# VectorE's convolution taps accumulate in two PSUM banks instead of two SBUF rows

## The chip, the cores and the metric

The kernel runs on one core of a Trainium2 chip. The metric is the device time of one execution in microseconds (us), the median of three runs. Engines are called by the names of the profile: PE is TensorE's matmul, PEld its weight load, DVE is VectorE, ACT is ScalarE, POOL is GpSimd, SP issues most DMAs.

## The reference

One decoder layer over 512 prompt tokens and 8 x 4 sampled tokens, 544 columns in all, model width 2048. An RMSNorm and one input projection give two groups. Group A is attention over keys that an indexer picks. Group B is a Conformer convolution module over 1024 channels; then an output projection, a SwiGLU FFN and a final norm. What the change touches is group B:

```python
def conformer_conv(u, conv_prev, conv_dw, conv_dw_bias, conv_ln_g, conv_ln_b):
    a, gate = jnp.split(u, 2, axis=-1)
    g = a * jax.nn.sigmoid(gate)
    buf = jnp.concatenate([conv_prev.astype(g.dtype), g], axis=1)
    y = lax.conv_general_dilated(buf, conv_dw[:, None, :].astype(buf.dtype), window_strides=(1,),
                                 padding='VALID', dimension_numbers=('NWC', 'WIO', 'NWC'),
                                 feature_group_count=CONV_WIDTH)
    y = jax.nn.silu(layer_norm(y + conv_dw_bias, conv_ln_g, conv_ln_b))
    return y, buf[:, -(CONV_KERNEL - 1):]
```

The convolution is depthwise and causal, 31 taps wide: each output column is the sum of 31 shifted columns of `g`, each times a weight of its channel. All data is fp32.

## The kernel before

Activations lie transposed, channels on partitions and tokens in the free dimension. Every weight tile (1024 rows by 128 columns, a "unit") is loaded by SP into one of four slots of `raw`, split by ScalarE into a high part (`whi`, L587) and by VectorE or GpSimd into the remainder (`wlo`, L848 and L516), and multiplied by TensorE in three products per half, 48 matmuls of 272 columns a unit (`unit`, L1346). A tile of 128 output channels is two units, and a pair is two tiles. Slot 0 of the accumulators is PSUM banks 0 and 1, slot 1 banks 2 and 3. ScalarE and the remainder work one pair ahead of TensorE.

The stage around the change runs over the eight blocks of 128 convolution channels (c = 0 to 7). Every engine has its own program, and semaphores join them.

- TensorE: for block i the first tile of the pair P_U + i (the values), then `new_state(i - 1)`, a transpose of the tile `tg` (L1477), then the second tile (the gates). It waits for `s_tg` before the transpose. After block 7 come the pairs P_Q (with the last transpose between its tiles), P_Q + 1, and then the column sums for the LayerNorm (L1494), which wait for all taps (`s_conv`).
- VectorE, `u_step(c)`: scale the values out of PSUM into `ga` (L1057); taps 0 to 9 of block c - 1 (`taps`, L1017 to L1024); scale the gates into `sg` (L1057), after a wait for TensorE's second tile; `convolved(c - 1)`, that is taps 10 to 20, the row sums of GpSimd's products for the sampled tokens (L1032, L1034), and two adds that join the partial sums (L1037, L1040); `gated(c)`, which writes the new `gbuf` and ends with `tg` (L1046 to L1054); one round of the sampled tokens' top-k (L1066 to L1069). The loop runs c = 1 to 7. The taps of block 7 lie in `rope_pair(P_Q)`, between and behind the two ropes. Before the loop there are seven top-k rounds.
- The 31 taps of a block are divided: VectorE has ND = 21 and ScalarE and GpSimd have NA = 10. ScalarE makes the product of one tap (L683, into `y2` or `tap`), GpSimd adds it to `y2` (L526, nine adds). GpSimd also makes the products of the sampled tokens (L534) and four remainders per block (L516), in between the adds, in the order of `conv_step`.
- VectorE's taps alternate between two accumulators, even taps in the row of `y` and odd ones in `y3`, both in SBUF. Tap k waits until tap k - 2 is complete (`s_conv`). Taps 0 and 1 are a multiply of `gbuf` with the weight, tap 0 with the bias added; the others are one instruction each, accumulator = `gbuf` shifted by k, times weight, plus accumulator (L1024).
- PSUM in this stage: banks 0 to 3 accumulate, bank 6 takes the transposes of `tg`. Banks 4 and 5 are used before it (the transposed old state, copied out by ScalarE, `s_stc`) and after it (the LayerNorm's squares, L1501).

Of the kernel before, what the change touches and what calls it, by code (L numbers as in the profile page):

```python
# [14 lines left out]
F32 = mybir.dt.float32  # L15
# [3 lines left out]
ALU = mybir.AluOpType  # L19
# [3 lines left out]
P = 128  # L23
D = 2048
SEQ = 512
# [24 lines left out]
NA = 10  # L50
# [66 lines left out]
def build(nc, a, o):  # L117
    with ExitStack() as ctx:
# [7 lines left out]
        def at(name, shape, dt, offset):  # L126
            return nc.alloc_sbuf_tensor_at(name, shape, dt, offset=base + offset)
# [10 lines left out]
        vec = at("vec", [P, 56], F32, C0 + 1280)  # L138
        cw = at("cw", [P, CT, CK], F32, C0 + 1504)
        stat = at("stat", [P, 64], F32, C0 + 2496)  # L140
        S0 = C0 + 2816
# [48 lines left out]
        gbuf = at("gbuf", [P, SEQ + CK - 1 + B * (CK - 1 + T)], F32, R0)  # L190
        y = at("y", [P, CT, NT], F32, R0 + 3264)
# [5 lines left out]
        cout = at("cout", [CK - 1 + NS, CW_], F32, S0 + 26880)  # L197
        tapS = at("tapS", [P, B, T, CK], F32, S0 + 17408)
        y2 = at("y2", [P, SEQ], F32, S0 + 21760)
        y3 = at("y3", [P, SEQ], F32, S0 + 23936)  # L200
        tap = at("tap", [P, 2, SEQ], F32, S0 + 49728)
        vT = at("vT", [P, NKV, NT], F32, S0 + 49728)
        kN = at("kN", [P, 5, 256], F32, S0 + 38848)
# [637 lines left out]
        def _(dve):  # L841
# [166 lines left out]
            ch.link(ve.tensor_copy(scK[:, :], scS[:, :]))  # L1008
            ve.memset(gbuf[:, 0:CK - 1], 0.0).then_inc(s_xs, 1)

            def taps(c, k0, k1):

                yp = y[:, bass.ds(c, 1), 0:SEQ].rearrange("p a n -> p (a n)")
                for k in range(k0, k1):
                    wk = cw[:, bass.ds(c, 1), k]
                    if k == 0:
                        ve.tensor_scalar(yp, gbuf[:, 0:SEQ], wk, vec[:, bass.ds(32 + c, 1)], ALU.mult, ALU.add  # L1017
                                         ).then_inc(s_conv, 1)
                    elif k == 1:
                        ve.tensor_scalar(y3[:, :], gbuf[:, 1:1 + SEQ], wk, None, ALU.mult).then_inc(s_conv, 1)  # L1020
                    else:
                        dst = y3[:, :] if k % 2 else yp
                        dve.wait_ge(s_conv, CN * c + k - 1)
                        ve.scalar_tensor_tensor(dst, gbuf[:, k:k + SEQ], wk, dst, ALU.mult, ALU.add  # L1024
                                                ).then_inc(s_conv, 1)

            def convolved(c):
# [6 lines left out]
                ve.tensor_scalar(ys, ys, vec[:, bass.ds(32 + c, 1)], None, ALU.add).then_inc(s_ssum, 1)  # L1034
                yp = y[:, bass.ds(c, 1), 0:SEQ].rearrange("p a n -> p (a n)")
                dve.wait_ge(s_conv, CN * c + ND)
                ve.tensor_tensor(yp, yp, y3[:, :], ALU.add).then_inc(s_conv, 1)  # L1037
                dve.wait_ge(s_conv, CN * c + ND + 1)
                dve.wait_ge(s_add, (NA - 1) * c + NA - 1)
                ve.tensor_tensor(yp, yp, y2[:, :], ALU.add).then_inc(s_conv, 1)  # L1040

            def gated(c):

# [687 lines left out]
```

## Time and profile before

| | |
|---|---|
| median of 3 runs | 2850.33 us (2847.47 to 2851.39) |
| profiled execution | 2844.5 us |
| its span | 2842.8 us |
| busy in the span: PE, PEld | 2613.4 us (92%), 2447.4 us (86%) |
| DVE, ACT, POOL | 1289.6 us (45%), 828.6 us (29%), 433.0 us (15%) |
| mean granted TensorE clock | 0.962 of full speed |
| chain that ended last, by engine | PE 79%, DVE 9%, issue 7% |

The span is the profiled execution without what lies around its first and last instruction, 1.7 us here. The convolution stage is from about 310 to 636 us of it and the FFN from about 1100 us to the end. A row of a timeline may stand for several equal instructions, with their count at its end; its second number then is from the start of the first to the end of the last. In brackets stands the idle time of the engine before it and who ended that.

### The profile page before, as it was taken

How to read it: one execution, taken by the hardware profiler on the slowest of the kernel's cores; microseconds unless marked ns; L12 is line 12 of the kernel's file. 1: busy time of each engine (PE TensorE's matmuls, PEld its weight loads, DVE VectorE, ACT ScalarE, POOL GpSimd, SP SyncE). 2: the span in 40 equal slices, each digit the busy share in tenths (PEclk: the TensorE clock that was granted, in tenths of full speed). 3: DMA queues.
4: the chain of work that ended last, by engine and by line, in shares of the span. 5: the costliest groups of instructions: out<-in, count | busy, mean ns of one | idle time of the engine just before them, and what ended most of it. 6: DMA issues, size and time to landing. Idle time of an engine off the chain costs nothing.

```text
span 2842.8 us, 50617 instructions
## 1 busy us (share of the span) xinstructions
PE 2613.4 (92%) x19388; PEld 2447.4 (86%) x19390; DVE 1289.6 (45%) x1750; ACT 828.6 (29%) x1052; POOL 433.0 (15%) x439
## 2 busy tenths in 40 slices
PE   5977877669889899999999999999999999999997
PEld 5952877669754479999999999999999999999997
DVE  5577599996561223343333333333333333333333
ACT  5143233222341212243332233322333322222222
POOL 3302477665323300000000000000000000000000
PEclk8988988889999999999999999999999999999999
DMA  7403222122325533423322333223322223333232
GB/s 223 110 3 87 60 56 55 52 78 56 91 86 162 158 101 108 132 77 89 89 70 84 104 89 89 85 67 89 105 88 83 76 81 100 90 88 89 68 89 98
DMA packets 424178, 256.01 MB, mean 90 GB/s; under 512 B 19915, under 2 KB 413235, under 8 KB 422752
## 3 DMA queue, kind: packets, MB, share of 16 engines
q1 hardware_dynamic: 412176, 225.88, 27.4%
q0 software_dynamic: 11936, 29.30, 3.5%
q8 instruction: 36, 0.59, 0.1%
q14 instruction: 30, 0.25, 0.0%
HBM read 244.70 MB, written 11.27 MB: 90 GB/s over the span
## 4 chain that ended last, share of the span: by engine, by line
PE 79%; DVE 9%; issue 7%; ACT 2%; DMA 1%; DVEq 1%; POOLq 0%; POOL 0%; SPq 0%; ACTq 0%
PE ps L1346 70%; DVE y L1024 2%; PE ps L1597 2%; PE ps L1626 2%; PE ps L1574 1%; DVE scP L957 1%; PE ps L1452 1%; DVE scS L1069 1%; PE ps L1428 0%; DVE m L1066 0%; DVE y L1017 0%; PE ps L1554 0%; ACT whi L587 0%; DVE stat L1207 0%; PE ps L1443 0%
## 5 line engine op out<-in xcount | busy, mean ns | idle before, releaser
L848 DVE TENSOR_TENSOR wlo<-raw,whi 128x1024 fp32r<-128x1024 f32 (+1 forms) x358 | 437.6, 1223 | 1192.5 <-ACT whi L587 1191.9
L1346 PE MATMUL ps<-xhi,whi 128*128 128x272 f32 (+1 forms) x4512 | 944.6, 291 | 15.0 <-DVE wlo L848 7.5
L1346 PE MATMUL ps<-xhi,wlo 128*128 128x272 f32 (+1 forms) x4512 | 939.0, 290 | 0.0
L1346 PE MATMUL ps<-xlo,whi 128*128 128x272 f32 (+1 forms) x4512 | 938.7, 290 | 0.0
L587 ACT CAST whi<-raw 128x1024 fp32r<-128x1024 f32 (+1 forms) x410 | 429.2, 1047 | 1286.0 <-PE ps L1346 1199.0
L1346 PEld LDWEIGHTS ps<-xhi,whi 128*128 128x128 f32 (+1 forms) x4512 | 715.9, 190 | 17.2 <-issue 10.8
L1346 PEld LDWEIGHTS ps<-xlo,whi 128*128 128x128 f32 (+1 forms) x4512 | 716.6, 190 | 0.0
L1346 PEld LDWEIGHTS ps<-xhi,wlo 128*128 128x128 f32 (+1 forms) x4512 | 711.6, 190 | 0.0
L1346 PE MATMUL ps<-hidh,whi 128*128 128x272 f32 x1408 | 291.4, 288 | 4.6 <-DVE hidl L1300 4.6
L1346 PE MATMUL ps<-hidl,whi 128*128 128x272 f32 x1408 | 290.9, 288 | 0.0
L1346 PE MATMUL ps<-hidh,wlo 128*128 128x272 f32 x1408 | 290.8, 288 | 0.0
L1346 PEld LDWEIGHTS ps<-hidh,whi 128*128 128x128 f32 x1408 | 219.5, 188 | 5.5 <-issue 5.5
L1346 PEld LDWEIGHTS ps<-hidl,whi 128*128 128x128 f32 x1408 | 219.7, 188 | 0.0
L1346 PEld LDWEIGHTS ps<-hidh,wlo 128*128 128x128 f32 x1408 | 219.6, 188 | 0.0
L1024 DVE SCALAR_TENSOR_TENSOR y<-gbuf,cw,y 128x512 f32<-128x512 f32 (+1 forms) x152 | 206.5, 1426 | 0.0
L516 POOL TENSOR_TENSOR wlo<-raw,whi 128x1024 fp32r<-128x1024 f32 x52 | 135.9, 2618 | 52.2 <-ACT whi L587 52.2
L526 POOL TENSOR_TENSOR y<-y,tap 128x512 f32<-128x512 f32 x72 | 112.3, 1559 | 3.5
L683 ACT ACTIVATE tap<-gbuf,cw 128x512 f32<-128x512 f32 x72 | 52.0, 722 | 98.3 <-POOL y L526 98.0
L1477 PE MATMUL ps<-ident,tg 128*128 128x128 f32 x8 | 3.6, 447 | 79.6 <-DVE tg L1054 79.6
L1477 PEld LDWEIGHTS ps<-ident,tg 128*128 128x128 f32 x8 | 1.4, 178 | 81.1 <-issue 68.9
L350 POOL DMA_DIRECT2D idxN<-in_cache_idx_k x96 | 51.7, 539 | 102.4 <-issue 101.5
L820 ACT CAST hidh<-ut 128x544 f32 x44 | 28.5, 647 | 128.5 <-DVE ut L1298 128.5
(278 smaller groups left out, 1752.3 us busy)
## 6 DMA issues: line engine op xcount, KB each, us to landing
raw<-in_w_gate SPq DMA_DIRECT2D x88, 512.0 KB, 3.8
raw<-in_w_up SPq DMA_DIRECT2D x88, 512.0 KB, 3.8
raw<-in_w_in SPq DMA_DIRECT2D x72, 512.0 KB, 3.8
raw<-in_w_down SPq DMA_DIRECT2D x64, 384.0 KB, 3.3
raw<-in_w_down SPq DMA_DIRECT2D x64, 320.0 KB, 3.1
raw<-in_w_out SPq DMA_DIRECT2D x32, 512.0 KB, 5.3
ring_pages<-in_cache_k SPq DMA_DIRECT2D x48, 128.0 KB, 2.7
ring_pages<-in_cache_k POOLq DMA_DIRECT2D x48, 128.0 KB, 3.1
```

Source lines behind the costliest of these rows:

```text
L350: eng.dma_start(idxN[:, b % IB, bass.ds(g, 1), :].rearrange("p a d -> p (a d)"), ic[bass.ds(pg, 1), :, :].rearrange("a s d -> (a s) d")).t ...
L516: nc.gpsimd.tensor_tensor(wlo[:, u.slot, :, :], raw[:, u.slot, :, :], whi[:, u.slot, :, :].bitcast(F32), ALU.subtract).then_inc(s_lo, 1)
L526: nc.gpsimd.tensor_tensor(y2[:, :], y2[:, :], tap[:, (k - 1) % 2, :], ALU.add).then_inc(s_add, 1)
L587: nc.scalar.copy(whi[:, u.slot, :, 0:cols], raw[:, u.slot, :, 0:cols]).then_inc(s_hi, 1)
L683: nc.scalar.activation(dst, gbuf[:, ND + k:ND + k + SEQ], ACT.Copy, scale=cw[:, bass.ds(c, 1), ND + k]).then_inc(s_tap, 1)
L820: nc.scalar.copy(tile_of(hidh, j), halves(ut[:, :])).then_inc(s_hh, 1)
L848: ve.tensor_tensor(wlo[:, u.slot, :, 0:cols], raw[:, u.slot, :, 0:cols], whi[:, u.slot, :, 0:cols].bitcast(F32), ALU.subtract).then_inc(s_ ...
L957: ve.scalar_tensor_tensor(dst, rel[:, n % 2, 0:SW[i]], wiP[:, i, hh:hh + 1], dst, ALU.mult, ALU.add).then_inc(s_ia, 1)
L1024: ve.scalar_tensor_tensor(dst, gbuf[:, k:k + SEQ], wk, dst, ALU.mult, ALU.add).then_inc(s_conv, 1)
L1346: ins = te.matmul(ps[0:cols, 2 * slot + half, 0:HALF], w[:, u.slot, t, 0:cols], x[:, k0 + t, HALF * half:HALF * half + HALF], start=(hf == ...
L1597: ins = te.matmul(ps[r0:r0 + 32, c, :], qpad[:, b, kv, :], kpT[:, q % 2, kv, :], start=False, stop=True, skip_group_check=True)
L1626: ins = te.matmul(ps[r0:r0 + 32, 7, 0:256], pST[:, 4 * (j % 4) + k, r0:r0 + 32], page_slot(n)[:, k, :], start=(j % 4 == 0 and k == 0), sto ...
```

## The change

The row `y3` goes. The even taps accumulate in PSUM bank 4 and the odd taps in bank 5. The two adds at the end change places: first odd taps plus `y2` into the row of `y`, after a wait for GpSimd's adds, and then even taps plus that row.

```diff
-        y3 = at("y3", [P, SEQ], F32, S0 + 23936)
...
+            even_taps, odd_taps = ps[:, 4, 0:SEQ], ps[:, 5, 0:SEQ]
+
             def taps(c, k0, k1):
 
-                yp = y[:, bass.ds(c, 1), 0:SEQ].rearrange("p a n -> p (a n)")
                 for k in range(k0, k1):
                     wk = cw[:, bass.ds(c, 1), k]
                     if k == 0:
-                        ve.tensor_scalar(yp, gbuf[:, 0:SEQ], wk, vec[:, bass.ds(32 + c, 1)], ALU.mult, ALU.add
+                        ve.tensor_scalar(even_taps, gbuf[:, 0:SEQ], wk, vec[:, bass.ds(32 + c, 1)], ALU.mult, ALU.add
                                          ).then_inc(s_conv, 1)
                     elif k == 1:
-                        ve.tensor_scalar(y3[:, :], gbuf[:, 1:1 + SEQ], wk, None, ALU.mult).then_inc(s_conv, 1)
+                        ve.tensor_scalar(odd_taps, gbuf[:, 1:1 + SEQ], wk, None, ALU.mult).then_inc(s_conv, 1)
                     else:
-                        dst = y3[:, :] if k % 2 else yp
+                        dst = odd_taps if k % 2 else even_taps
                         dve.wait_ge(s_conv, CN * c + k - 1)
                         ve.scalar_tensor_tensor(dst, gbuf[:, k:k + SEQ], wk, dst, ALU.mult, ALU.add
                                                 ).then_inc(s_conv, 1)
...
                 dve.wait_ge(s_conv, CN * c + ND)
-                ve.tensor_tensor(yp, yp, y3[:, :], ALU.add).then_inc(s_conv, 1)
+                dve.wait_ge(s_add, (NA - 1) * c + NA - 1)
+                ve.tensor_tensor(yp, odd_taps, y2[:, :], ALU.add).then_inc(s_conv, 1)
                 dve.wait_ge(s_conv, CN * c + ND + 1)
-                dve.wait_ge(s_add, (NA - 1) * c + NA - 1)
-                ve.tensor_tensor(yp, yp, y2[:, :], ALU.add).then_inc(s_conv, 1)
+                ve.tensor_tensor(yp, even_taps, yp, ALU.add).then_inc(s_conv, 1)
```

The order of VectorE's program at the end of a block, in `convolved` and the start of `gated`, before the change (`y_113` is `y3`, `y_112` is `y2`, a wait stands in brackets):

```order
L1034 TENSOR_SCALAR y<-y,vec 128x32 [waits s_ssum]
L1036 REGISTER_ALU
L1037 TENSOR_TENSOR y<-y,y_113 128x512 [waits s_conv]
L1038 REGISTER_ALU
L1039 ISA [waits s_conv]
L1040 TENSOR_TENSOR y<-y,y_112 128x512 [waits s_add]
L1045 REGISTER_ALU
L1046 ISA [waits s_conv]
L1046 COPY gbuf<-stT 128x8x30
```

The same place in the changed kernel (`ps` is PSUM):

```order
L1034 TENSOR_SCALAR y<-y,vec 128x32 [waits s_ssum]
L1036 REGISTER_ALU
L1037 ISA [waits s_conv]
L1038 ISA [waits s_add]
L1038 TENSOR_TENSOR y<-ps,y_112 128x512
L1039 REGISTER_ALU
L1040 TENSOR_TENSOR y<-ps,y 128x512 [waits s_conv]
L1045 REGISTER_ALU
L1046 ISA [waits s_conv]
L1046 COPY gbuf<-stT 128x8x30
```

The wait for GpSimd's adds stands ahead of the first of the two adds instead of the second. Nothing else changes its place on any engine; the taps keep their order and change only their operands.

## Rows read from the trace of the kernel before

**Rows 1.** Waits of TensorE, 357 to 588 us: who waited for whom, total, times, longest

```profile
PE ps L1477 <- DVE tg L1054: 67.6, 6, 12.7
```

**Rows 2.** Stretches: length; busy PE, PEld, DVE, ACT, POOL (instructions); clock; DMA share; GB/s

```profile
357.00:395.50 38.50, 27.11 (x193) 26.87 (x193) 37.55 (x38) 11.50 (x16) 27.79 (x17) 0.81 0.21 55
...
1100.00:2800.00 1700.00, 1690.18 (x13474) 1688.64 (x13473) 581.51 (x604) 495.26 (x502) 0.00 (x0) 1.00 0.30 88
```

**Rows 3.** Timeline of VectorE, one step: start, length, line, instruction

```profile
395.27 0.17 DVE L1054 COPY tg<-gbuf 128x32 f32<-128x32 f32 x1
...
398.34 1.53 DVE L1017 TENSOR_SCALAR y<-gbuf,cw,vec 128x512 f32 x1
399.79 2.62 DVE L1020 TENSOR_SCALAR y<-gbuf,cw 128x512 f32<-128x512 f32 x1
402.33 15.91 DVE L1024 SCALAR_TENSOR_TENSOR y<-gbuf,cw,y 128x512 f32 x8
418.17 0.71 DVE L1057 TENSOR_TENSOR sg<-ps,rstd 128x544 f32<-128x544 f32 x1
418.80 10.93 DVE L1024 SCALAR_TENSOR_TENSOR y<-gbuf,cw,y 128x512 f32 x11
429.66 1.17 DVE L1032 TENSOR_REDUCE y<-tapS 128x992 f32 x1
...
431.02 0.68 DVE L1037 TENSOR_TENSOR y<-y,y 128x512 f32 x1
...
433.79 0.17 DVE L1054 COPY tg<-gbuf 128x32 f32<-128x32 f32 x1
```

**Rows 4.** Timeline of VectorE, first step of the loop (taps 0, 1, 2 to 9)

```profile
336.80 2.25 DVE L1017 TENSOR_SCALAR y<-gbuf,cw,vec 128x512 f32 x1
338.96 0.47 DVE L1020 TENSOR_SCALAR y<-gbuf,cw 128x512 f32<-128x512 f32 x1
339.36 5.38 DVE L1024 SCALAR_TENSOR_TENSOR y<-gbuf,cw,y 128x512 f32 x8
```

**Rows 5.** Timeline of GpSimd, same two steps

```profile
336.39 2.36 POOL L516 TENSOR_TENSOR wlo<-raw,whi 128x1024 fp32r<-128x1024 f32 x1
...
395.72 2.62 POOL L534 TENSOR_TENSOR tapS<-gbuf,cw 128x248 f32<-128x248 f32 x4 [10.36 <-DVE tg L1054]
...
415.95 5.17 POOL L526 TENSOR_TENSOR y<-y,tap 128x512 f32<-128x512 f32 x3
421.09 2.80 POOL L516 TENSOR_TENSOR wlo<-raw,whi 128x1024 fp32r<-128x1024 f32 x1
```

**Rows 6.** Timeline of VectorE, first rope add of P_Q

```profile
592.23 2.83 DVE L916 TENSOR_TENSOR qT<-qT,rt 128x544 f32<-128x544 f32 x1
```

**Rows 7.** Groups of VectorE by line and shape: count, busy us, mean ns

```profile
L1310 DVE TENSOR_TENSOR h<-ps,h 128x544 f32 x62 | 44.4, 716 | 0.0
...
L1298 DVE TENSOR_TENSOR ut<-ut,gt 128x544 f32<-128x544 f32 x44 | 31.9, 726 | 7.9 <-DVE ut L1295 6.6
...
L1207 DVE TENSOR_REDUCE stat<-ps 128x1 f32<-128x512 f32 x8 | 5.5, 689 | 5.2 <-PE ps L1536 5.2
...
L1207 DVE TENSOR_REDUCE stat<-ps 128x1 f32<-128x128 f32 x8 | 2.3, 287 | 0.1
```

**Rows 8.** Single lines: shortest, median and longest duration in ns

```profile
L1024 DVE SCALAR_TENSOR_TENSOR y<-gbuf,cw,y x152: 729/1156/5904, 339.4 to 632.6; 128x512 f32<-128x512 f32 x82, 128x512 f32 x70
...
L526 POOL TENSOR_TENSOR y<-y,tap x72: 1263/1628/1768, 317.1 to 611.6; 128x512 f32<-128x512 f32 x72
...
L516 POOL TENSOR_TENSOR wlo<-raw,whi x52: 2357/2578/2872, 293.2 to 730.1; 128x1024 fp32r<-128x1024 f32 x52
```

**Rows 9.** Timeline of TensorE after the transpose of `tg`

```profile
395.79 0.82 PE L1346 MATMUL ps<-xhi,whi 128*128 128x272 f32 x2
```

**Rows 10.** Timeline of TensorE after the convolution: column sums, next pair

```profile
636.06 9.27 PE L1494 MATMUL ps<-y,ones 128*128 128x272 f32 x32 [7.81 <-DVE y L1040]
646.57 0.52 PE L1346 MATMUL ps<-xhi,whi 128*128 128x272 f32 x2 [1.24 <-DVE rt L913]
```

## The prediction

> **What bounds the kernel now.** I began with the waits of TensorE in the stretch of the convolution. Between 357 and 588 us it waits for one thing, the tile `tg` that VectorE's gated() writes: six times, 67.6 us in all [rows 1]. The table of stretches then shows the two sides of one step (one channel block, about 38.5 us): VectorE is busy 37.55 us of it, TensorE 27.11 us, and TensorE's granted clock is 0.81 there, against 1.00 in the FFN [rows 2]. So VectorE sets the length of a step and TensorE waits. The step is read from VectorE's timeline: from `tg` to the next `tg` is 433.79 - 395.27 = 38.52 us, of which the first ten taps take 398.34 to 418.17 and the other eleven 418.80 to 429.66 [rows 3].
>
> The taps are what is slow. In the first step of the loop GpSimd's last instruction ends at 338.75, and taps 2 to 9, from 339.36 on, take 5.38 us, 0.67 us each [rows 4, 5]. In a steady step GpSimd works (2.62 us of products at 395.72, then adds and weight remainders until 423.9) and the same eight taps take 15.91 us, 2.0 us each [rows 3, 5]. A tap reads `gbuf` and its accumulator, both in SBUF. At 418.17 VectorE runs `sg<-ps,rstd`, one operand of which is in PSUM, in the middle of three GpSimd adds (415.95 to 421.12), and it takes 0.71 us, as ever [rows 3, 5]. At 592.23 a rope add with both operands in SBUF takes 2.83 us [rows 6]; alone such an instruction takes 0.73 [rows 7]. So an instruction with two SBUF tensors waits for GpSimd's, and one with a single SBUF tensor does not. The Trainium skill (SBUF — State Buffer, "Who interferes with whom") says that VectorE's second SBUF input comes through a port shared with GpSimd, held for a whole instruction, the loser blocked; by that rule the trace agrees, 2.0 us against 0.67.
>
> **The change, part by part.** Taps 2 to 20 keep one operand in SBUF (`gbuf`) and move the other, with the result, to PSUM banks 4 and 5. No instruction is added or removed. No other engine touches those banks between the last state copy and the squares of the LayerNorm.
>
> *Price of a tap, p.* No row shows VectorE writing PSUM. The nearest, an add that reads PSUM and SBUF, takes 0.716 us for 544 columns, the same with both in SBUF 0.726 [rows 7]: reading PSUM is free. The low end is 0.67 us, the tap without GpSimd [rows 4]; a gain on that is excluded, since its 512 columns take the time that they take in any row, PSUM or SBUF. In the middle lies 0.73, the shortest duration recorded of one tap [rows 8]: now a tap starts 0.06 us before the one ahead of it has ended, and in PSUM it might not. The high end is 1.2 us, if reading and writing one bank take turns: from 128 to 512 columns a reduction out of PSUM goes from 0.287 to 0.689 us [rows 7], so 512 columns are worth 0.53 us, which would come twice. I take p = 0.70, between the two that it resembles most, since reading PSUM shows no price; 1.2 stays as a rival. The Trainium skill (VectorE: DVE Perf Modes, "The TRN2 errata") gives a VectorE instruction from PSUM 62 cycles more than one from SBUF, an estimate of 0.065 us a tap. By it p would be 0.735 and the kernel some 3 us slower than my sum; the two adds of [rows 7] show nothing of it, and no row here has a write to PSUM. Taps 0 and 1 read only `gbuf` plus scalars; they took 1.5 and 2.6 us beside GpSimd [rows 3]. I price them at p too.
>
> *The new steady step*, counted from the end of `tg` (395.44 in rows 3):
> - TensorE's second tile starts 0.35 us after it (395.79) [rows 9] and has 96 matmuls. At full clock one takes 1690.18 / 13474 = 0.1254 us [rows 2], so 12.0 us; with 0.2 us until VectorE sees it, `sg` can be read at 12.6.
> - VectorE reaches its first tap at 2.9 (398.34) and ends ten at 2.9 + 10p = 9.9. It now waits 2.7 us for TensorE, a wait that the old trace does not have.
> - `sg` 0.63, eleven taps 11p = 7.7: at 20.9. The sum of the sampled products and its bias take 431.02 - 429.66 = 1.36: at 22.3 the two adds begin. From there to the end of `tg` takes 433.96 - 431.02 = 2.94.
> - Together 17.5 + 11p = 25.2 us.
>
> *What is late next.* GpSimd must have made its nine adds by 22.3: it starts at 0.3, then 2.6 for the products, 9 x 1.26, and three remainders of 2.36 by their shortest durations [rows 5, 8]: 21.3. The add wait is moved ahead of both sums instead of one, but it has 1.0 us to spare. The last remainder ends at 23.7, before the copies into `gbuf` at 24.0, so these don't collide. TensorE needs 0.35 + 192 x 0.1254 = 24.4: it waits 0.8 us a step. ScalarE has 11.50 us of work a step [rows 2] and its products only follow GpSimd's adds. The weight loads, a DMA share of 0.21 over 38.5 us, become 0.32 over 25.2, what the FFN holds without a wait (0.30) [rows 2]. Three engines within a microsecond: below 24.4 the step cannot go.
>
> *Sum.* Steps 2 to 7: 6 x (38.52 - 25.2) = 79.9 us. TensorE enters the first of them from the idle time before tg(1) at the lower clock: after a wait of 11 us (67.6 / 6) [rows 1] its first pair of matmuls takes 0.82 us [rows 9], against 0.52 after a short wait [rows 10], which makes 27.11 us out of 24.4 with the transpose [rows 2]; that costs 2.7 once. The first step gains 1.6 on tap 0 (2.25 now) and loses 0.2 on tap 1 (0.47 now) and 19 x 0.03 on the rest: 0.8 [rows 4]. After tg(7) at 588.0 the last block lies between the two ropes of P_Q. TensorE runs P_Q's second tile to 600.5, P_Q+1 to 624.6 at full clock, no longer held by the second rope; VectorE begins the taps 7 us after tg(7), as now: the first rope's add keeps its two SBUF operands and its wait [rows 6]. Ten taps bring it to 602, the second rope with such an add (some 4.7) to 606.7, eleven taps to 614.4, product sums and adds (1.4 + 1.4) to 617. So the 7.81 us wait at 636.06 goes [rows 10], the column sums start at 624.6, take 9.3 and end at 633.9. VectorE needs 646.57 - 636.06 = 10.5 us from the end of its sums until its top-k rounds and the rope have freed bank 0 [rows 10], so that is at 628 and in time. P_Q+2 starts at 633.9 where it started at 646.57: 12.7 us. Behind it the same engines wait for each other in the same order, up to an FFN bound by TensorE, so nothing gives this back.
>
> 0.8 + 79.9 - 2.7 + 12.7 = 90.7 us. The profiled execution took 2844.5 us, so 2753.8; the median of the three runs is 5.8 above it, so 2759.6, say **2759 us**.
>
> **The rivals.**
> 1. *TensorE's clock does not recover* (or GpSimd turns out 2 us late). For it: it was 0.81 in the step of [rows 2]. Against: the falls follow waits of 11 us, and a wait of 1.24 us at 646.57 is followed by a pair of matmuls in 0.52 us where after the long wait it took 0.82 [rows 9, 10]. If each short wait cost the 2.7 us, the step is 28 us and the kernel 6 x 2.7 = 16 slower: 2775.
> 2. *PSUM in place is slow,* p = 1.2. Then VectorE is the chain throughout: 7.8 + 21p = 33.0 a step, 33 us gained there, about 9 behind tg(7), 9.6 lost in the first step, which has no GpSimd to hide from: 2850 - 32 = 2818. For it: no row has such a write. Against: reading PSUM costs nothing.
> 3. *Slower: the taps stay blocked.* Every tap also reads a per-partition scalar of `cw` from SBUF. If that read, and not the second tensor, is what waits for GpSimd, taps take as long as now, (418.17 - 398.34 + 429.66 - 418.80) / 21 = 1.46 us on average [rows 3], and each is longer by what PSUM adds to it, 0.06 us at p = 0.73: 21 x 8 blocks x 0.06 = 10 us, so 2860. It decides from p = 1.46, where 7.8 + 21p reaches 38.5. Against: ropes and `sg` do not show it, but they have no such scalar.
> 4. *The change does nothing*, the taps not being on the path: 2850. Rows 1 and 2 speak plainly against it.
>
> **How the numbers follow.** The forecast has 0.80, rival 1 has 0.08, rival 2 0.06, rival 3 0.05, rival 4 0.01. The forecast's own range: p from 0.67 to 0.73 gives steps of 24.9 to 25.5 and TensorE's floor 24.4, so 2754 to 2761, and with 4 us for the tail and the spread of runs 2749 to 2768. To hold rival 1 the range goes up to 2780 and leaves out rivals 2 to 4, 0.12. Measured differences under 0.2% (5.7 us) are no change: same is 0.01, slower 0.05 by rival 3, faster 0.94.
>
> **What would show it.** In the new profile taps of 0.67 to 0.75 us in every step; VectorE waiting about 2.7 us for TensorE before `sg`; GpSimd's adds at 1.27 us instead of 1.6, since nothing makes them wait either; `tg` every 25 us; TensorE's granted clock near 1 from 395 us on; no wait before the column sums; and the end moved by what the stretch up to 650 us gained. Taps over 1 us would prove rival 2 (the same length in the first step) or 3 (short in the first step, long later). A step of 28 us with TensorE's clock at 0.8 is rival 1. I am wrong if the step shortens and the end does not follow.

## The result and the profile after

| | before | after |
|---|---|---|
| median | 2848.9 us (2847.05 to 2851.39, 4 runs) | 2758.12 us (2757.81 to 2762.01, 4 runs) |
| profiled execution, its span | 2844.5, 2842.8 us | 2758.33, 2756.6 us |
| busy PE | 2613.4 us (92%) | 2605.8 us (95%) |
| busy DVE, POOL | 1289.6, 433.0 us | 1177.1, 404.3 us |
| mean granted TensorE clock | 0.962 | 0.975 |
| `tg(1)` to `tg(7)` | 231.1 us | 154.1 us |

The ratio is 0.9684 (0.9667 to 0.9701): 90.8 us less by the medians, where 90.7 were forecast, and 0.9 us from the forecast time. As a difference of the two profiled executions it is 86.2 us. That these are two numbers is part of the explanation below. The kernel before stands at 2850.33 us in the table of its own profile, by three runs; a fourth, of 2847.05 us, brings its median to 2848.9.

The costliest groups of the changed kernel's page, those of the taps and of GpSimd's adds (busy us, mean ns of one, idle time before):

```profile
L1024 DVE SCALAR_TENSOR_TENSOR ps<-gbuf,cw,ps 128x512 f32<-128x512 f32 x152 | 101.5, 748 | 0.0
L525 POOL TENSOR_TENSOR y<-y,tap 128x512 f32<-128x512 f32 x72 | 94.2, 1308 | 3.5
```

All 152 taps now last between 741 and 755 ns, where the old ones went from 729 to 5904 [rows 8]. GpSimd's adds got shorter as well, 1308 ns on average (median 1304) after a median of 1628: the two engines had been holding each other up.

One step of VectorE in the changed kernel, `tg` to `tg`, which answers to [rows 3]. It is 405.85 - 380.43 = 25.42 us long:

```profile
380.43 0.17 DVE L1054 COPY tg<-gbuf 128x32 f32<-128x32 f32 x1
...
383.50 0.81 DVE L1017 TENSOR_SCALAR ps<-gbuf,cw,vec 128x512 f32<-128x512 f32 x1
384.22 0.75 DVE L1020 TENSOR_SCALAR ps<-gbuf,cw 128x512 f32<-128x512 f32 x1
384.87 5.36 DVE L1024 SCALAR_TENSOR_TENSOR ps<-gbuf,cw,ps 128x512 f32<-128x512 f32 x8
393.28 0.72 DVE L1057 TENSOR_TENSOR sg<-ps,rstd 128x544 f32<-128x544 f32 x1 [3.05 <-PE ps L1346]
393.92 7.33 DVE L1024 SCALAR_TENSOR_TENSOR ps<-gbuf,cw,ps 128x512 f32<-128x512 f32 x11
...
402.37 0.24 DVE L1034 TENSOR_SCALAR y<-y,vec  x1
402.67 0.69 DVE L1038 TENSOR_TENSOR y<-ps,y 128x512 f32 x1
403.39 0.69 DVE L1040 TENSOR_TENSOR y<-ps,y 128x512 f32 x1
404.23 0.78 DVE L1046 COPY gbuf<-stT 128x240 f32 x1
...
405.85 0.17 DVE L1054 COPY tg<-gbuf 128x32 f32<-128x32 f32 x1
```

The eight taps that took 15.91 us take 5.36. Taps 0 and 1 are short too, although they read one SBUF tensor as before and only their result has moved. Tap 1 in all eight blocks, before and after (shortest, median, longest in ns):

```profile
L1020 DVE TENSOR_SCALAR y<-gbuf,cw x8: 475/2610/2617, 339.0 to 596.4; 128x512 f32<-128x512 f32 x8
```

```profile
L1020 DVE TENSOR_SCALAR ps<-gbuf,cw x8: 737/744/747, 335.4 to 515.4; 128x512 f32<-128x512 f32 x8
```

Before `sg` VectorE waits 3.05 us for TensorE. GpSimd in the same step, for [rows 5]:

```profile
380.88 2.64 POOL L533 TENSOR_TENSOR tapS<-gbuf,cw 128x248 f32<-128x248 f32 x4 [3.07 <-DVE tg L1054]
...
387.08 4.06 POOL L525 TENSOR_TENSOR y<-y,tap 128x512 f32<-128x512 f32 x3
...
398.46 4.06 POOL L525 TENSOR_TENSOR y<-y,tap 128x512 f32<-128x512 f32 x3
402.48 2.39 POOL L515 TENSOR_TENSOR wlo<-raw,whi 128x1024 fp32r<-128x1024 f32 x1
```

Its ninth add is through at 402.5 and VectorE's first sum starts at 402.67: these two are as good as level. And the last remainder, 402.48 to 404.87, lies over the copy at 404.23, which takes 0.78 us instead of 0.28.

Waits of TensorE from 357 to 510 us, where 67.6 us stood before [rows 1], and the stretch of one step for [rows 2]:

```profile
PE ps L1477 <- DVE tg L1054: 5.0, 6, 0.9
```

```profile
381.50:406.90 25.40, 24.51 (x195) 24.23 (x194) 21.48 (x38) 11.38 (x18) 23.59 (x18) 1.00 0.26 66
```

TensorE is busy 24.51 of 25.40 us at full clock. VectorE is no longer the fullest engine (21.48); GpSimd (23.59) is fuller than it.

### The profile page after: what moved, and what is told of

It is laid out like the page before. It is cut to its first block, busy times and chain, and to the rows that moved or that the text cites. A ratio compares the mean times of both kernels' runs of the same rounds, so it can differ in the third digit from the quotient of the medians.

```text
span 2756.6 us, 50626 instructions
## 1 busy us (share of the span) xinstructions
PE 2605.8 (95%) x19390; PEld 2438.2 (88%) x19390; DVE 1177.1 (43%) x1750; ACT 827.7 (30%) x1052; POOL 404.3 (15%) x439
## 4 chain that ended last, share of the span: by engine, by line
PE 86%; DVE 6%; issue 3%; ACT 2%; DMA 1%; POOL 1%; DVEq 0%; SPq 0%; POOLq 0%; ACTq 0%
PE ps L1346 76%; PE ps L1597 2%; PE ps L1626 2%; PE ps L1574 1%; DVE scP L956 1%; POOL y L525 1%; PE ps L1452 1%; PE ps L1428 1%; DVE ps L1024 1%; PE ps L1554 0%; PE ps L1443 0%; ACT whi L586 0%; ACT idxT L651 0%; PE ps L1536 0%; DVE stat L1207 0%
## 5 line engine op out<-in xcount | busy, mean ns | idle before, releaser
L515 POOL TENSOR_TENSOR wlo<-raw,whi 128x1024 fp32r<-128x1024 f32 x52 | 125.4, 2416 | 49.2 <-ACT whi L586 49.2
L1024 DVE SCALAR_TENSOR_TENSOR ps<-gbuf,cw,ps 128x512 f32<-128x512 f32 x152 | 101.5, 748 | 0.0
L525 POOL TENSOR_TENSOR y<-y,tap 128x512 f32<-128x512 f32 x72 | 94.2, 1308 | 3.5
L1597 PE MATMUL ps<-kpT,qpad 128*32 128x512 f32 x128 | 62.6, 615 | 0.0
L1250 DVE COPY kpT<-ps 128x512 f32<-128x512 f32 x32 | 22.1, 691 | 71.4 <-PE ps L1574 71.4
```

The costliest lines, as they stand in the source:

```text
L515: nc.gpsimd.tensor_tensor(wlo[:, u.slot, :, :], raw[:, u.slot, :, :], whi[:, u.slot, :, :].bitcast(F32), ALU.subtract).then_inc(s_lo, 1)
L525: nc.gpsimd.tensor_tensor(y2[:, :], y2[:, :], tap[:, (k - 1) % 2, :], ALU.add).then_inc(s_add, 1)
L1597: ins = te.matmul(ps[r0:r0 + 32, c, :], qpad[:, b, kv, :], kpT[:, q % 2, kv, :], start=False, stop=True, skip_group_check=True)
```

## The experiments

**One operand at a time.** The prediction rested on one statement: what makes a tap slow is the second *read* from SBUF, and not the write to SBUF. The change moves both. The first two runs move one each.

`e1_read_psum`, made from the changed kernel: the taps read their accumulator in PSUM and write to the rows in SBUF. They no longer accumulate; the sum over the taps is left out.

```diff
+        y3 = at("y3", [P, SEQ], F32, S0 + 23936)
...
+                yp = y[:, bass.ds(c, 1), 0:SEQ].rearrange("p a n -> p (a n)")
...
-                        ve.scalar_tensor_tensor(dst, gbuf[:, k:k + SEQ], wk, dst, ALU.mult, ALU.add
+                        row = y3[:, :] if k % 2 else yp
+                        ve.scalar_tensor_tensor(row, gbuf[:, k:k + SEQ], wk, dst, ALU.mult, ALU.add
...
-                ve.tensor_tensor(yp, odd_taps, y2[:, :], ALU.add).then_inc(s_conv, 1)
+                ve.tensor_tensor(yp, yp, y3[:, :], ALU.add).then_inc(s_conv, 1)
...
-                ve.tensor_tensor(yp, even_taps, yp, ALU.add).then_inc(s_conv, 1)
+                ve.tensor_tensor(yp, yp, y2[:, :], ALU.add).then_inc(s_conv, 1)
```

> Made from the changed kernel. Taps 2 to 20 read their second operand from PSUM but write their result to the SBUF rows of before, so they do not accumulate: the sum over the taps is left out, the number and size of the instructions is not. Theory A (what waits for GpSimd is the second SBUF tensor that is read): taps of 0.67 to 0.75 us beside GpSimd, a step of 25 to 26 us, 2756 to 2762 us. Rival theory B (what waits is the write of the result to SBUF, or a write to SBUF and a read from it together): taps of 1.4 to 2.0 us on average, a step of 38 us, about 2850 us.

2764.36 us, ratio 0.9713 (0.9685 to 0.9741). VectorE in a step:

```profile
396.41 7.32 DVE L1027 SCALAR_TENSOR_TENSOR y<-gbuf,cw,ps 128x512 f32 x11
...
405.12 2.85 DVE L1041 TENSOR_TENSOR y<-y,y 128x512 f32 x1
```

Taps that write SBUF are as short as those of the change: all 152 last between 731 and 747 ns. The step is 27.05 us, above the 25 to 26 expected and the change's 25.4, because this kernel's sum of the two rows reads two SBUF tensors again: it starts beside GpSimd's last remainder and takes 2.85 us.

`e2_write_psum`, the reverse, made from the kernel before: taps 2 to 20 read the rows in SBUF and write PSUM. The sum over the taps is left out here too, and the two adds stand as in the changed kernel.

```diff
+            even_taps, odd_taps = ps[:, 4, 0:SEQ], ps[:, 5, 0:SEQ]
...
-                        dst = y3[:, :] if k % 2 else yp
+                        dst = odd_taps if k % 2 else even_taps
                         dve.wait_ge(s_conv, CN * c + k - 1)
-                        ve.scalar_tensor_tensor(dst, gbuf[:, k:k + SEQ], wk, dst, ALU.mult, ALU.add
+                        row = y3[:, :] if k % 2 else yp
+                        ve.scalar_tensor_tensor(dst, gbuf[:, k:k + SEQ], wk, row, ALU.mult, ALU.add
...
-                ve.tensor_tensor(yp, yp, y3[:, :], ALU.add).then_inc(s_conv, 1)
+                dve.wait_ge(s_add, (NA - 1) * c + NA - 1)
+                ve.tensor_tensor(yp, odd_taps, y2[:, :], ALU.add).then_inc(s_conv, 1)
                 dve.wait_ge(s_conv, CN * c + ND + 1)
-                dve.wait_ge(s_add, (NA - 1) * c + NA - 1)
-                ve.tensor_tensor(yp, yp, y2[:, :], ALU.add).then_inc(s_conv, 1)
+                ve.tensor_tensor(yp, even_taps, yp, ALU.add).then_inc(s_conv, 1)
```

> The mirror image: taps 2 to 20 read their second operand from the SBUF rows and write to the PSUM banks; the sum over the taps is left out here too. Theory A: the taps wait for GpSimd as before, 2.0 us each while it runs, a step of 38 to 39 us, about 2850 us. Theory B: taps of 0.67 to 0.75 us and 2756 to 2762 us. If a write to PSUM costs something of its own, it shows in the first step, where GpSimd is idle: over 0.67 us a tap there.

2847.99 us, ratio 0.9995 (0.9984 to 1.0006): nothing is left of the gain. Its first step, which has no GpSimd beside it, and a later one:

```profile
339.14 5.39 DVE L1027 SCALAR_TENSOR_TENSOR ps<-gbuf,cw,y 128x512 f32<-128x512 f32 x8
...
401.98 15.94 DVE L1027 SCALAR_TENSOR_TENSOR ps<-gbuf,cw,y 128x512 f32<-128x512 f32 x8
```

15.94 us, as before the change [rows 3], with the result in PSUM. The first step has them in 5.39 us, so the write to PSUM costs nothing by itself. Both runs together: for an instruction with two tensor inputs, the gain is in the read.

**Half of the taps.** `e3_odd_only`: only the odd taps have PSUM, the even ones stay in `y`.

```diff
-                        ve.tensor_scalar(even_taps, gbuf[:, 0:SEQ], wk, vec[:, bass.ds(32 + c, 1)], ALU.mult, ALU.add
+                        ve.tensor_scalar(yp, gbuf[:, 0:SEQ], wk, vec[:, bass.ds(32 + c, 1)], ALU.mult, ALU.add
...
-                        dst = odd_taps if k % 2 else even_taps
+                        dst = odd_taps if k % 2 else yp
...
-                ve.tensor_tensor(yp, odd_taps, y2[:, :], ALU.add).then_inc(s_conv, 1)
+                ve.tensor_tensor(yp, odd_taps, yp, ALU.add).then_inc(s_conv, 1)
...
-                ve.tensor_tensor(yp, even_taps, yp, ALU.add).then_inc(s_conv, 1)
+                ve.tensor_tensor(yp, yp, y2[:, :], ALU.add).then_inc(s_conv, 1)
```

> Half of the change: the odd taps accumulate in PSUM bank 5, the even ones in the row of y as before. Theory A: every second tap still waits for GpSimd and delays one of its instructions in turn; the other runs in its shadow. Even taps of 1.2 to 2 us, odd ones of 0.75 us, the first ten taps in about 10 to 13 us instead of 20; a step of 28 to 32 us, 2775 to 2805 us. Rival (no lock, but the two accumulators in neighbouring SBUF rows disturb each other, so that one in PSUM is enough): all taps short and 2758 us.

2803.24 us, ratio 0.985 (0.9821 to 0.9878), a step of 31.1 us. Even and odd taps in one step, and the bias of the sampled row:

```profile
391.20 2.22 DVE L1025 SCALAR_TENSOR_TENSOR y<-gbuf,cw,y 128x512 f32 x1
393.35 0.74 DVE L1025 SCALAR_TENSOR_TENSOR ps<-gbuf,cw,ps 128x512 f32<-128x512 f32 x1
394.01 1.12 DVE L1025 SCALAR_TENSOR_TENSOR y<-gbuf,cw,y 128x512 f32 x1
...
412.17 2.36 DVE L1035 TENSOR_SCALAR y<-y,vec  x1
```

All even and all odd taps of the run:

```profile
L1025 DVE SCALAR_TENSOR_TENSOR y<-gbuf,cw,y x80: 736/1124/7690, 337.7 to 579.0; 128x512 f32 x70, 128x512 f32<-128x512 f32 x10
L1025 DVE SCALAR_TENSOR_TENSOR ps<-gbuf,cw,ps x72: 741/743/751, 338.3 to 578.3; 128x512 f32<-128x512 f32 x72
```

Side by side in one step, the odd taps take 0.74 us and the even ones 1.12 or more, but for one of 0.74 that began 0.11 us ahead of a GpSimd add. A per-partition scalar from `cw` stands in both, so it is not what waits. The bias L1035 is a surprise that returns below: this instruction has a single SBUF tensor as its input, and it waited too.

**The other side of the contention.** `e4_short_adds`: the kernel before, with GpSimd's adds cut to one of 512 columns (their sum is left out).

```diff
-                    nc.gpsimd.tensor_tensor(y2[:, :], y2[:, :], tap[:, (k - 1) % 2, :], ALU.add)
+                    nc.gpsimd.tensor_tensor(y2[:, 0:1], y2[:, 0:1], tap[:, (k - 1) % 2, 0:1], ALU.add)
```

> Made from the kernel before, with VectorE's taps in SBUF. GpSimd's nine adds per block are cut to one column each, with all their waits and signals; their sum is left out for the other 511 columns. The remainders and the sampled products stay. Theory A: only the taps that meet a remainder (four of 2.4 us per block) wait; a step of 25 to 29 us, 2765 to 2790 us. Rival (the taps are slow in SBUF for a reason other than GpSimd): a step of 36 us or more and over 2830 us.

2789.96 us, ratio 0.9803 (0.9773 to 0.9833). The old taps (shortest, median, longest in ns):

```profile
L1024 DVE SCALAR_TENSOR_TENSOR y<-gbuf,cw,y x152: 733/741/2897, 336.4 to 562.2; 128x512 f32<-128x512 f32 x82, 128x512 f32 x70
```

Without touching VectorE's program the median tap falls from 1156 to 741 ns and the step to 29.9 us, where 25 to 29 were expected. What is left to the changed kernel's step, 4.5 us, goes with taps beside the remainders: eight taps take 9.68 us at 389.92, with two remainders among them, against 5.36. So it is GpSimd's instructions that made the taps slow.

**The add order.** `e5_early_wait`: the kernel before, with the changed order of the two adds and its earlier wait alone.

```diff
-                ve.tensor_tensor(yp, yp, y3[:, :], ALU.add).then_inc(s_conv, 1)
-                dve.wait_ge(s_conv, CN * c + ND + 1)
                 dve.wait_ge(s_add, (NA - 1) * c + NA - 1)
-                ve.tensor_tensor(yp, yp, y2[:, :], ALU.add).then_inc(s_conv, 1)
+                ve.tensor_tensor(y3[:, :], y3[:, :], y2[:, :], ALU.add).then_inc(s_conv, 1)
+                dve.wait_ge(s_conv, CN * c + ND + 1)
+                ve.tensor_tensor(yp, yp, y3[:, :], ALU.add).then_inc(s_conv, 1)
```

> The other part of the change alone, in the kernel before: accumulators stay in SBUF, but the wait for GpSimd's adds stands ahead of the first of the two sums, which now adds y2 to the odd row. Theory: GpSimd is done some 8 us before VectorE comes to the sums, so the earlier wait costs nothing: 2849 us, within 3 us of the kernel before. Rival: the earlier wait or the other order of the sums is worth something by itself: 2840 us or less, or 2855 us or more.

2849.42 us, ratio 1.0006 (0.9996 to 1.0015): in the kernel before, the order and the earlier wait are worth nothing. What the earlier wait costs in the changed kernel, where GpSimd's ninth add ends just ahead of the first sum, this run can't show.

**Who sets the new step?** `e6_split14`: the changed kernel with 14 instead of 10 taps ahead of `sg`, so that VectorE works in the 3 us in which it waits.

```diff
-                taps(c, ND // 2, ND)
+                taps(c, 14, ND)
...
-                     mid=(lambda: taps(c - 1, 0, ND // 2)) if conv else None, lows=False)
+                     mid=(lambda: taps(c - 1, 0, 14)) if conv else None, lows=False)
...
-            rope_pair(P_Q, qT, 0, 9, c1, s1, HD, mid=lambda: taps(CT - 1, 0, ND // 2), lows=False)
+            rope_pair(P_Q, qT, 0, 9, c1, s1, HD, mid=lambda: taps(CT - 1, 0, 14), lows=False)
```

> The changed kernel, with 14 instead of 10 taps ahead of the wait for TensorE's second tile, and 7 behind it. They fit into the 3.05 us that VectorE waits there. Theory (GpSimd's adds end with VectorE's last tap, both chains decide): VectorE is ready 2.6 us earlier and waits for GpSimd instead; a step still of 25.2 to 25.4 us, 2757 to 2759 us. Rival (VectorE's taps behind TensorE's tile are the only chain): a step down to TensorE's 24.4 us, 6 us less: 2752 us.

2758.14 us, ratio 0.9691 (0.9678 to 0.9704), a step of 25.37 us: no gain. VectorE comes to the bias L1034 2.6 us earlier, is held there for up to 1.36 us (three of the six steps have the usual 0.24), and then waits for GpSimd at its first sum (waits from 357 to 510 us):

```profile
DVE y L1038 <- POOL y L525: 10.9, 5, 2.7
```

GpSimd sets the end of the step as much as VectorE does.

`e7_na9` takes a tap from ScalarE and GpSimd instead and gives it to VectorE.

```diff
-NA = 10
+NA = 9
```

> The changed kernel with one tap moved from ScalarE and GpSimd (NA 9 for 10) to VectorE (22 for 21), 11 ahead of TensorE's tile, 11 behind it as now. Theory: GpSimd ends 1.37 us earlier, its last remainder no longer stands in the way of the copy into gbuf (0.5 us), VectorE's chain stays: a step of 24.8 us, 3 to 4 us less, 2754 to 2755 us. Rival (only VectorE's chain): no change, 2758 us; if the tap more costs VectorE its 0.66 us on the path, 2762 us.

2760.09 us, ratio 0.9697 (0.9684 to 0.9711), a step of 25.65 us, where 24.8 and 2754 to 2755 us were expected. This was a miss. GpSimd is 1.4 us sooner at its last remainder, 402.69 for a `tg` at 382.06, and VectorE runs into that:

```profile
404.00 1.11 DVE L1034 TENSOR_SCALAR y<-y,vec  x1
```

0.24 us in the changed kernel's steady steps, 1.10 to 1.16 here in five steps. The bias of 32 columns has one tensor input, in SBUF, and its result in SBUF, and it waits for GpSimd to end.

`e8_na9_split14` is both edits together.

> Both edits together: 22 taps on VectorE, 14 ahead of TensorE's tile and 8 behind, GpSimd with eight adds. Theory: both chains end before TensorE is ready, TensorE waits for tg no longer, a step of 24.4 us from the third on: 6 us less than the changed kernel, 2752 us. If a third chain holds the step (ScalarE, the weight loads), it stays above 24.8 us and the time at 2754 us or more.

2749.76 us, ratio 0.9654 (0.9641 to 0.9668): 8.4 us faster than the change. Its short steps are 24.0 us (402.96 to 426.95 to 450.98), in which TensorE never waits: that is 192 matmuls at 0.125 us, and less than the 24.4 that the prediction and this run's theory took for the floor. Two of the six steps are longer. The first is 25.67 us: TensorE enters it after a wait of 5.74 us, and its granted clock over it is 0.92. The fifth is 25.71 us at full clock: in it the bias L1034 takes 2.44 us beside a remainder. The next experiment is about the first of these causes, the last three about the second.

**The start of the stage.** What still held TensorE was VectorE's late arrival at the first `ga` and `tg(1)` (waits of 3.0 and 5.2 us in the changed kernel). `e9_early3`, made from `e8_na9_split14`, starts 3 rounds of the sampled top-k before the loop instead of 7 and does the other four later.

```diff
-EARLY = 7
+EARLY = 3
...
-            topk_sample(R1, 3)
-            R1 += 3
+            topk_sample(R1, 5)
+            R1 += 5
             rope_pair(P_K, kT, 0, 17, c1, s1, HD, lows=False)
-            topk_sample(R1, 3)
-            R1 += 3
+            topk_sample(R1, 5)
+            R1 += 5
```

> The run before it (nine taps on GpSimd, fourteen of VectorE's taps ahead of sg, steps of 24.0 us), and in addition only 3 steps of the later side work are begun ahead of the convolution instead of 7, and two samples behind it take 5 steps each instead of 3. Theory (what still holds TensorE at the start of the first stage is VectorE coming late to ga(1) and tg(1)): VectorE comes to ga(1) some 10 us sooner, TensorE no longer waits 3.0 us for ga and 5.2 us for tg(1), and does not fall to the low clock there; 10 to 12 us less than the run before, so 2738 to 2742. Rival (the work that was begun early is wanted later, and its delay holds up the rotary embedding and attention): what the first stage gains is given back there, 2748 or more. Second rival: the moved work stands inside the steps on VectorE, each step longer than 24.0 us; then tg(1) to tg(7) is over 146 us and the time about 2745 to 2750.

2740.29 us, ratio 0.9618 (0.9604 to 0.9631), 9.5 us less than the run before it and inside the first theory's 2738 to 2742. `tg(0)` to `tg(1)` fell from 41.2 to 30.3 us, and 1.6 us of it is given back between `tg(7)` and the sampled attention. The first step, 345.44 to 371.16, is still 25.72 us long: in it the bias L1034 takes 2.36 us. All waits of TensorE for `tg` from 300 to 620 us:

```profile
PE ps L1477 <- DVE tg L1054: 0.4, 1, 0.4
```

**A second profile of the changed kernel.** `e10_after_again`, no edit.

> The changed kernel once more, for a second profile of it. Theory: the length of the sampled-attention stage (188.7 us at a granted clock of 0.93 in the changed kernel's profile, 182.3 us at 0.96 in the profile before) belongs to an execution and not to the change, since runs with the old taps show both; so this profile may show either, and its profiled time is some 6 us lower where it shows the short one (2752). Rival: the changed taps bring the stage its length; then it is 188 to 189 us again, and the profiled time 2757 to 2760.

2762.01 us (2761.26 to 2764.22), ratio 0.9697 (0.9682 to 0.9713), profiled 2761.78. The long sampled-attention stage was there again, so this run does not tell theory and rival apart. The rival falls by other runs, below; the theory stays open. What it showed instead are two steps of 27.0 us behind the first, at 406 and at 433 us. VectorE and GpSimd at the end of the first:

```profile
427.94 2.47 DVE L1034 TENSOR_SCALAR y<-y,vec  x1
```

```profile
427.98 2.39 POOL L515 TENSOR_TENSOR wlo<-raw,whi 128x1024 fp32r<-128x1024 f32 x1
```

and TensorE at the start of a normal step (406.31) and of the one behind it (433.30):

```profile
406.31 0.32 PE L1477 MATMUL ps<-ident,tg 128*128 128x128 f32 x1 [0.90 <-DVE tg L1054]
406.51 0.51 PE L1346 MATMUL ps<-xhi,whi 128*128 128x272 f32 x2
...
433.30 0.40 PE L1477 MATMUL ps<-ident,tg 128*128 128x128 f32 x1 [2.47 <-DVE tg L1054]
433.51 0.82 PE L1346 MATMUL ps<-xhi,whi 128*128 128x272 f32 x2
```

In the other steady steps of this kernel's two profiles the bias starts 0.06 to 0.12 us ahead of the remainder and is through in 0.24 us. Here the two are 0.04 us apart, and it takes 2.47, the remainder's whole length: `tg` comes late, TensorE waits 2.47 us, and it goes on at the lower of its two clocks, 1.2 GHz (0.87 of full speed granted over 433 to 446.5 us), which makes the next step 26.95 us too. A margin of less than a tenth of a microsecond decides over 3.1 us, nearly all of the 3.45 us between the two profiled executions of this kernel (2761.78 and 2758.33).

**Out of the way of it.** The last two runs let the row sum of the sampled products write 32 columns of PSUM bank 7, where the bias reads them. `e11_na9_psum_reduce` is `e7_na9` with this.

```diff
-                ve.reduce_sum(ys, tapS[:, :, :, :].rearrange("p b t k -> p (b t) k"), AX.X).then_inc(s_ssum, 1)
+                yr = ps[:, 7, 0:NS]
+                ve.reduce_sum(yr, tapS[:, :, :, :].rearrange("p b t k -> p (b t) k"), AX.X).then_inc(s_ssum, 1)
                 dve.wait_ge(s_ssum, 2 * c + 1)
-                ve.tensor_scalar(ys, ys, vec[:, bass.ds(32 + c, 1)], None, ALU.add).then_inc(s_ssum, 1)
+                ve.tensor_scalar(ys, yr, vec[:, bass.ds(32 + c, 1)], None, ALU.add).then_inc(s_ssum, 1)
```

> The run with nine taps on GpSimd (steps of 25.65 us, in which the bias of the sampled row, L1034, took 1.10 to 1.16 us beside GpSimd's last remainder in five of them), with the row sum of the sampled products written to 32 columns of PSUM bank 7 and the bias reading it there; nothing else. Theory (an instruction of VectorE that reads one tensor from SBUF and writes SBUF waits for GpSimd's too, and L1034 is the one that does here): L1034 takes 0.3 us or less in every step and in the last block, where it took 3.83; the steps fall to about 24.8 us, tg(1) to tg(7) from 154.7 to 150 us, and the time by 4 to 5 us to some 2755.5. Rival (the wait has nothing to do with where L1034 reads: the write to SBUF, or the wait for the reduction ahead of it, is what is slow): L1034 stays at 1.1 us and the steps at 25.65. Second rival: L1034 is short, but the wait goes to the next instruction (the first of the two adds, or the copy of the old state into gbuf), and the steps stay above 25.4.

2755.15 us, ratio 0.9664 (0.9651 to 0.9678), 4.9 us less than `e7_na9`. The bias in all eight blocks (first fence, this run) and in `e7_na9` (second):

```profile
L1035 DVE TENSOR_SCALAR y<-ps,vec x8: 249/250/251, 353.4 to 534.4; 128x32 f32 x7, 128x32 f32<-128x32 f32 x1
```

```profile
L1034 DVE TENSOR_SCALAR y<-y,vec x8: 241/1122/3835, 352.6 to 536.4; - x7, 128x32 f32<-128x32 f32 x1
```

0.25 us in every block. The step is 25.06 us and not 24.8: a wait of 0.17 us for the row sum has come ahead of the bias, and `tg(1)` to `tg(7)` fell by 2.8 us where 4.7 were expected. The rest of the 4.9 us lies outside this stretch or in the spread of the runs.

`e12_early3_psum_reduce` is `e9_early3` with the same edit.

> The fastest so far (nine taps on GpSimd, fourteen taps ahead of sg, three early steps: 2740.29 us, steps of 24.0 us but one of 25.72, where L1034 took 2.36), with the row sum of the sampled products in PSUM as in the run beside it. Theory: L1034 takes 0.3 us in every step; the step of 25.72 us becomes 24.0 to 24.1 too, tg(1) to tg(7) 144 to 145 instead of 145.9 us, and the time falls by 1.5 to 2 us, to 2738 to 2739, which the runs can hardly tell from no change; the step table is the test. Rival as in the run beside it: L1034 over 0.3 us in some step, and a step over 25 us with it.

2739.97 us, ratio 0.9614 (0.9601 to 0.9627): by its time no different from `e9_early3`. The steps are what was expected, 24.01 to 24.17 us all six (144.6 us together, after 145.9), without the one of 25.72. This is the fastest version of the study, 108 us below the kernel before; the change gave 91 of it.

## Why the prediction was right

By its steps, with the balance of the two profiled executions:

| stretch | forecast | measured |
|---|---|---|
| ahead of `tg(0)` | 0 | 2.1 us |
| `tg(0)` to `tg(1)` | 0.8 | 1.2 |
| `tg(1)` to `tg(7)` | 79.9 - 2.7 = 77.2 | 231.1 - 154.1 = 77.0 |
| `tg(7)` to P_Q+2 | 12.7 | 58.7 - 43.6 = 15.1 |
| behind it | 0 | -9.2 |
| sum | 90.7 | 86.2 |

That the medians differ by 90.8 us where 90.7 were forecast is in part luck. In the profiled executions the stretches up to P_Q+2 gained 95.4 us, 4.7 more than forecast, and 9.2 us were given back where the forecast had nothing. The 2.1 us ahead of `tg(0)` are spread and not the change: in the profiles whose program is the same up to there, `tg(0)` lies anywhere from 309.8 to 315.0 us. The second measurement of the same kernel (`e10_after_again`) lies 3.9 us higher, at 2762.01.

**What bounded the kernel, and the second operand: right, and shown.** The steps shortened by what the forecast said. `e1_read_psum` and `e2_write_psum` put what taps 2 to 20 gained on the second read from SBUF, and `e4_short_adds` on GpSimd as the other party. The Trainium skill (SBUF — State Buffer, "Who interferes with whom") has the same rule, that a VectorE instruction with two SBUF inputs contends with a GpSimd instruction that reads SBUF; the trace agrees, and `e2_write_psum` adds that for such an instruction it does not matter where the result goes.

**The price of a tap: inside the range, a little high.** Taken was 0.70 us; start to start it is 5.36 - 0.08 = 5.28 us for eight, 0.66. In the prediction's terms that is the low end: a tap in PSUM still starts ahead of the end of the one before. Ahead of `sg` the shorter taps only made the wait longer (3.05 us, forecast 2.7); behind it they brought the first sum to 22.1 us (402.67 - 380.60), where 22.3 was forecast. The Trainium skill (VectorE: DVE Perf Modes, "The TRN2 errata") would have 62 cycles more for an instruction from PSUM; in these taps, 748 ns against 741 for undisturbed ones in SBUF (`e4_short_adds`), no such amount is seen.

**The steady step: 25.2 forecast, 25.4 measured, with errors in GpSimd's part and in the floor.** "21.3 [...] it has 1.0 us to spare" took the shortest add of the old trace, 1.26 us. The adds come 1.35 us apart (4.06 us for three), so the ninth ends at 21.9 us, and 0.15 us was the whole margin; `e6_split14` shows that GpSimd is an equal bound there. "The last remainder ends at 23.7, before the copies into `gbuf` at 24.0, so these don't collide": it ends at 24.3 and the copies begin at 23.6 (404.23 - 380.60), and the first takes 0.78 us instead of 0.28. From the start of the first sum to the end of `tg` it takes 3.35 us (402.67 to 406.02) instead of the 2.94 of the sum; the taps' 0.2 us make up for half of that. "Below 24.4 the step cannot go" was too high: the 0.35 us from `tg` to TensorE's next tile was counted in it, and where `tg` is early TensorE does not wait for it. Steps of 23.98 to 24.09 us in `e8_na9_split14` and `e9_early3` show it.

**The rule behind it was too narrow.** "An instruction with two SBUF tensors waits for GpSimd's, and one with a single SBUF tensor does not": the second half rested on `sg`, whose big operand is in PSUM. A multiply, add or copy with one tensor from SBUF to SBUF waits as well: the bias L1034 in `e3_odd_only`, `e7_na9` and `e10_after_again`, the copy L1046 in the changed kernel. With the operand moved to PSUM the bias stopped waiting, though it still writes SBUF (`e11_na9_psum_reduce`). Taps 0 and 1 are the other way round: they still read `gbuf` in SBUF, write PSUM, and last 802 to 806 and 737 to 747 ns in all eight blocks, beside GpSimd too. So of an instruction with one tensor input either end in PSUM was enough here, and of one with two inputs only the read. The rows on record had shown the wait: taps 0 and 1, each with `gbuf` alone, took 1.53 and 2.62 us beside GpSimd [rows 3], and the prediction priced them rightly without drawing the conclusion. The same section of the Trainium skill says that a copy or a multiply or add of one tensor, in the mode in which it uses both port pairs, blocks and is blocked for the whole instruction; the trace agrees with 2.47 us for an instruction of 0.24. The same section of the Trainium skill also says that reductions never contend on this chip, and L1032 took 1.17 to 1.19 us in every block of every run, beside GpSimd or not.

**The clock: right in kind.** The step behind `tg(1)`, entered after a wait of 5.23 us, was 27.05 instead of 25.41 us, so the term "2.7 once" was 1.64: the forecast took the loss of a step entered after 11 us. That term was too large by 1.1 us, and the steady steps, longer by 0.2 us each than forecast, offset it. After waits of 0.9 us the clock stays up.

**Behind the convolution: a size off.** The wait ahead of the column sums went, and they began 36.5 us behind `tg(7)`, where 36.6 was forecast. But they were priced at their old 9.3 us. Without a wait before them TensorE stays at full clock:

```profile
543.97 7.49 PE L1494 MATMUL ps<-y,ones 128*128 128x272 f32 x32
```

7.49 us, 1.8 us less, and the next pair starts in their last 0.35 us.

**"Nothing gives this back": 9.2 us are gone in the profiled executions, and the medians do not show them.** 6.4 us of them lie in one place, the sampled-attention stage (from its first page transpose to the last transpose of its output). The stretch before the change, after it, then in `e5_early_wait` (old taps) and in `e7_na9` (new ones):

```profile
836.40:1018.70 182.30, 162.56 (x735) 76.80 (x731) 34.55 (x46) 33.02 (x54) 52.45 (x96) 0.96 0.51 151
```

```profile
742.10:930.80 188.70, 168.78 (x736) 79.45 (x731) 34.53 (x46) 33.02 (x54) 52.45 (x96) 0.93 0.49 146
```

```profile
834.40:1022.90 188.50, 168.61 (x735) 79.39 (x731) 34.48 (x46) 33.06 (x54) 52.62 (x96) 0.93 0.49 146
```

```profile
747.60:930.10 182.50, 162.68 (x736) 76.84 (x731) 34.66 (x46) 33.06 (x54) 52.62 (x96) 0.96 0.50 150
```

The other engines are as busy to 0.2 us; TensorE has 6 us more work of the same instructions, at a lower clock. Both lengths exist with old taps and with new ones, so it is not the taps. Of the fourteen profiles of this study four have the short length (the kernel before, `e1_read_psum`, `e2_write_psum`, `e7_na9`); the other ten are 4 to 6 us longer, at 0.93 or 0.94. The profiled execution of the kernel before had the short one, and it was 4.4 us below its own median; the changed kernel's two had the long one, and the first lies at its median. This would fit a length that belongs to the execution, with the long one the usual case, and would explain why the medians differ by the full 90.8 us. Against it, `e2_write_psum` and `e7_na9` had the short one too and were profiled only 0.7 and 1.3 us below their medians. Shown is only that it is not the taps: each kernel but this one has one profile, so whether the execution decides or the kernel's timing stays open. Of the rest, 1.2 us lie between P_Q+2 and this stage and 1.7 behind it; no cause was looked for.

**The rivals.** Rival 1 (the clock does not recover) did not decide this kernel, but its mechanism is real: `e10_after_again` has it in one step, behind a wait of 2.47 us, in a step that is 1.5 us longer than usual, not 2.7. Rival 2 (PSUM in place is slow) falls by the 741 to 755 ns of all taps. Rival 3 (the scalar of `cw` waits) falls by the odd taps of `e3_odd_only`, 741 to 751 ns with that scalar. Rival 4 (the taps are not on the path) falls by the result.

## What to carry to other kernels

Where VectorE and GpSimd work side by side in SBUF, look in VectorE's timeline for instructions whose duration is not one of their usual values: those with two SBUF tensors, and copies or scalar multiplies and adds from SBUF to SBUF. Move one read into PSUM, also for tiny ones; the write may stay where it is. For an instruction with one tensor input, moving the result instead did as well (taps 0 and 1). Then count the other engine again with its new rate and not with its shortest rows: here a margin that was computed as 1.0 us was 0.15, and one of about 0.1 us, between a 32-column instruction and a remainder, costs 3 us whenever it is missed.

## What the hardware showed that was not expected

- A bias of 32 columns, 0.24 us, took 2.47 us when it began 0.04 us ahead of GpSimd's instruction in the records. In `e7_na9`'s last block it took 3.83 us, from 536.41 to 540.24, while GpSimd made two remainders in a row, from 535.44 to 540.20: the gap between them did not let it through. In `e6_split14`'s last block the same bias took 5.13 us, and in `e3_odd_only`'s an even tap took 7.69 us, from 570.69 on, with three remainders in a row from 570.72 to 577.82. The length of the blocked instruction says nothing about the length of the block.
- The second tap, with one tensor input, takes 0.47 us from SBUF to SBUF when it is alone [rows 4] and 0.75 us into PSUM. Out of GpSimd's way it is slower than alone, and still far from the 2.62 us that it took beside it [rows 3].
- In `e10_after_again` a step that was 1.6 us too long on VectorE made the next one 1.5 us too long as well: TensorE's clock was low after the wait of 2.47 us that it caused.
- The same 735 or 736 TensorE instructions of the sampled-attention stage took 182.3 to 188.7 us, with the work of all other engines unchanged.
